# An fp32 encoder trunk: first products without the wait for lambda constants, first weight chunks rounded on ScalarE, and output additions each followed by a square addition and a split

## What is computed

```
h = _rms(x, attn_norm[l])
z = h @ w_in[l]
...
lam = (jnp.exp(jnp.sum(lam_q1[l].astype(jnp.float32) * lam_k1[l].astype(jnp.float32)))
       - jnp.exp(jnp.sum(lam_q2[l].astype(jnp.float32) * lam_k2[l].astype(jnp.float32)))
       + lam_init)
y_diff = _diff_attention(dq, dk, dv, lam, diff_subln[l], lam_init)
...
y_mla = _mla_attention(q_nope, q_pe, k_nope, k_pe, v)

x = x + jnp.concatenate([y_diff, y_mla], axis=-1) @ w_o[l]

h = _rms(x, ffn_norm[l])
x = x + (jax.nn.silu(h @ w_gate[l]) * (h @ w_up[l])) @ w_down[l]
```

## Time and profile before

| | |
|---|---|
| median of 3 runs | 2512.65 us (2512.34 to 2515.03) |
| the profiled execution's own time | 2514.26 us |
| its span in the profile | 2512.5 us |
| mean granted TensorE clock | 0.986 |
| TensorE matmul busy | 2410.7 us, 96% of the span |
| VectorE, ScalarE, GpSimd busy | 1317.1, 564.0, 935.5 us |
| DMA queue q1 | 247.52 MB, 29.1% of 16 engines |

### The profile page before, as it was taken

One profiled execution on the slowest core, in us unless ns is written; L12 is line 12 of the kernel. 1 busy time (PEld: TensorE's weight loads), 2 busy tenths in 40 slices (PEclk: granted clock), 3 DMA queues, 4 the chain that ended last, 5 costly groups with the idle time before them and its releaser, 6 DMA issues.

```text
span 2512.5 us, 31147 instructions
## 1 busy us (share of the span) xinstructions
PE 2410.7 (96%) x11304; PEld 2002.7 (80%) x11304; DVE 1317.1 (52%) x2369; ACT 564.0 (22%) x1089; POOL 935.5 (37%) x798
## 2 busy tenths in 40 slices
PE   5989999989999999999999999999899999999996
PEld 4777788868888888888888888878688888888885
DVE  4898568874333333333359874896533333333335
ACT  2344234520000000000024531453100000000001
POOL 6534300155666666665110010003544343444421
PEclk9999999999999999999999999999899999999998
DMA  7543442232333333332232134223211111111101
GB/s 257 174 145 101 151 151 101 85 118 93 125 126 125 125 125 125 116 114 63 75 112 106 68 126 176 101 84 118 67 42 50 42 50 50 50 50 50 49 18 67
DMA packets 50345, 249.52 MB, mean 99 GB/s; under 512 B 5968, under 2 KB 6096, under 8 KB 32720
## 3 DMA queue, kind: packets, MB, share of 16 engines
q1 hardware_dynamic: 49536, 247.52, 29.1%
q10 hardware_dynamic: 720, 0.86, 0.1%
HBM read 187.54 MB, written 60.82 MB: 99 GB/s over the span
## 4 chain that ended last, share of the span: by engine, by line
PE 87%; DVE 5%; issue 2%; POOL 1%; ACT 0%; DVEq 0%; POOLq 0%; ACTq 0%
PE bank L449 28%; PE bank L451 27%; PE bank L450 27%; PE bank L805 2%; PE bank L668 1%; DVE acc L1150 1%; PE bank L676 1%; DVE aT_lo L1364 1%; DVE qpe L1243 1%; PE bank L456 0%; PE bank L455 0%; DVE y_out L1440 0%; ACT aT_hi L1030 0%; DVE ms L1185 0%; DVE mx L1356 0%
## 5 line engine op out<-in xcount | busy, mean ns | idle before, releaser
L449 PE MATMUL bank<-h_hi,w 128*128 128x512 f32 x1792 | 704.9, 393 | 2.6 <-issue 1.7
L451 PE MATMUL bank<-h_hi,w 128*128 128x512 f32 x1792 | 700.3, 391 | 0.0
L450 PE MATMUL bank<-h_lo,w 128*128 128x512 f32 x1792 | 700.1, 391 | 0.0
L574 POOL TENSOR_TENSOR w<-raw,zero 128x512 fp32r<-128x512 f32 x318 | 335.8, 1077 | 814.6 <-PE bank L451 756.9
L579 POOL TENSOR_TENSOR w<-raw,w 128x512 fp32r<-128x512 f32 x318 | 416.3, 1330 | 12.5
L449 PEld LDWEIGHTS bank<-h_hi,w 128*128 128x128 f32 x1792 | 338.4, 189 | 72.9 <-issue 3.8
L451 PEld LDWEIGHTS bank<-h_hi,w 128*128 128x128 f32 x1792 | 338.0, 189 | 71.3
L450 PEld LDWEIGHTS bank<-h_lo,w 128*128 128x128 f32 x1792 | 338.5, 189 | 69.4
L1408 DVE TENSOR_TENSOR x<-x,bank 128x512 f32<-128x512 f32 x352 | 239.9, 687 | 187.2 <-PE bank L451 184.1
L449 PE MATMUL bank<-u_hi,w 128*128 128x512 f32 x704 | 273.9, 389 | 0.0
L450 PE MATMUL bank<-u_lo,w 128*128 128x512 f32 x704 | 273.9, 389 | 0.0
(11 more groups left out here) (162 smaller groups left out, 3331.6 us busy)
## 6 DMA issues: line engine op xcount, KB each, us to landing
w<-parked SPq DMA_DIRECT2D x81, 1024.0 KB, 4.8
raw<-in_wffn SPq DMA_DIRECT2D x132, 512.0 KB, 3.5
parked<-w SPq DMA_DIRECT2D x27, 1024.0 KB, 6.4
parked<-p SPq DMA_DIRECT2D x27, 1024.0 KB, 4.8
raw<-in_watt SPq DMA_DIRECT2D x27, 512.0 KB, 4.3
praw<-in_watt SPq DMA_DIRECT2D x27, 512.0 KB, 5.7
out_yT<-y_out SPq DMA_DIRECT2D x16, 256.0 KB, 2.3
x<-in_xT SPq DMA_DIRECT2D x4, 512.0 KB, 6.7
```

What stands on the lines that cost most here:

```text
L449: nc.tensor.matmul(out_ap, lhs[0], rhs[0], start=first, stop=False)
L450: nc.tensor.matmul(out_ap, lhs[0], rhs[1], start=False, stop=False)
L451: return nc.tensor.matmul(out_ap, lhs[1], rhs[0], start=False, stop=last)
L574: last = nc.gpsimd.tensor_tensor(w[slot][0][:, cols], src[:, cols], zeros_like(src[:, cols]), ALU.add)
```

## The change

It has three parts.

1. TensorE's wait for s_load and for the set-up is taken from before V of layer 0, input 0, and put behind it, ahead of its first sums; it now asks s_pre for 2 (the ones and the zero) and not for the constants.
2. ScalarE rounds chunks 0, 1 and 2 (`first_hi`), behind x_hi of tiles 1, 3 and 7, and does all 8 squares after that. GpSimd only makes their lo parts. VectorE does all 8 x_lo first, and then the 8 square additions.
3. In input 1 of both layers VectorE does, behind each addition ob(k), k = 1 to 7, `square_add` and `x_lo` of tile k-1. Behind the table only those of tile 7 are left.

```diff
-            for c in (s_hi, s_lo, s_add):
+            for c in (s_lo, s_add):
...
-            def split(j, slot, raw_at, hi_at):
+            def split(j, slot, raw_at, hi_at, rounded=False):
...
-                for n, cols in enumerate(spans(2)):
-                    last = nc.gpsimd.tensor_tensor(w[slot][0][:, cols], src[:, cols], zeros_like(src[:, cols]), ALU.add)
-                last.then_inc(s_hi.sem, 1)
+                if not rounded:
+                    for n, cols in enumerate(spans(2)):
+                        last = nc.gpsimd.tensor_tensor(w[slot][0][:, cols], src[:, cols], zeros_like(src[:, cols]), ALU.add)
+                    last.then_inc(s_hi.sem, 1)
...
-                split(j, j % WS_ATT, s_raw[j % RAW].half_at(0, 0, j // RAW), s_hi.half_at(0, 0, j))
+                split(j, j % WS_ATT, s_raw[j % RAW].half_at(0, 0, j // RAW), s_hi.half_at(0, 0, j), j < 3)
...
-            pe.wait_ge(s_load, 4 * 16)
-            pe.wait_ge(s_pre, PRE_DVE)
...
                             values(l, b)
+                            if l == 0 and b == 0:
+                                pe.wait_ge(s_load, 4 * 16)
+                                pe.wait_ge(s_pre, 2)
...
+            def first_hi(j):
+                act.wait_ge(s_raw[j % RAW].sem, s_raw[j % RAW].half_at(0, 0, j // RAW))
+                for cols in spans(2):
+                    last = nc.scalar.activation(w[j][0][:, cols], raw[:, j % RAW, cols], ACT.Copy)
+                last.then_inc(s_hi.sem, 1)
+
             for k in range(KT):
                 x_hi("first", 0, 0, k)
+                if k in (1, 3):
+                    first_hi(k // 2)
+            first_hi(2)
+            for k in range(KT):
                 norm_square("first", 0, 0, k)
...
             for k in range(KT):
                 x_lo("first", 0, 0, k)
+            for k in range(KT):
                 square_add("first", 0, k)
...
                             add_output(l, b, what)
+                            if b == 1 and what[1] == "b" and what != "ob0":
+                                square_add("last", l, int(what[2]) - 1)
+                                x_lo("last", l, 0, int(what[2]) - 1)
...
-                for k in range(KT):
-                    square_add("last", l, k)
-                    x_lo("last", l, 0, k)
+                square_add("last", l, KT - 1)
+                x_lo("last", l, 0, KT - 1)
```

## The result

| | before | changed |
|---|---|---|
| median | 2512.49 us (2510.4 to 2515.03, 4 runs) | 2490.03 us (2487.16 to 2490.61, 4 runs) |
| ratio to before | | 0.9909, 95% interval 0.9897 to 0.9921 |
| the profiled execution's own time | 2514.26 us | 2487.16 us |
| its span | 2512.5 us | 2485.4 us |
| mean granted TensorE clock | 0.986 | 0.989 |

The kernel is 22.5 us faster. I had forecast about 2475, which is 37.5 less, with a range of 2468 to 2484: the sign is right, the size is not, and the time lies outside the range.

What follows compares the result with a forecast made beforehand. TensorE, busy 2410.7 of 2512.5 us, was taken to bound the kernel, with three stalls totalling 53.3 us. Gains of 18.0 + 9.9 + 9.9 = 37.8 took 2514.3 to 2476.5, the median to about 2475; range 2468 to 2484.

Steps and rivals of the forecast that it cites:

- The start: Kernel start: TensorE begins near 12.4 instead of 30.4 us, and the first sums come at 36.4; gain 18.0 us.
- rival 3: Start: chunks 3 and 4 land late, TensorE stands 2 to 4 us and pays 2.3 of clock; 2480, chance 0.08.
- the sum: Whole kernel: 18.0 us from the start plus 9.9 from each of two hand-overs, 37.8 in all.
- The lag of VectorE: Hand-overs: interleaved work makes the last output addition 2.4 us late, so TensorE stands 3.3 us before the FFN's first product.
- rival 2: Hand-overs: VectorE lags 5.7 us, stall 6.6, gain only 6.6 each, total 31; 2481, chance 0.14.
- The low clock behind them: Hand-overs: after the stall before the FFN's first product the clock falls, costing 2.3 us over the 48 products.
- The step that failed: Hand-overs: sums at once, 0.9, then 24 products, 5.4, to 564.0 instead of 573.83; gain 9.9 us each.
- Rival 1: Hand-overs: the clock doesn't fall at the FFN's start; gain 12.2 each, total 42.4, 2470, chance 0.17.
- Rival 4: Hand-overs: TensorE waits before each ob product at 1.2 GHz, losing 17.4 us per hand-over; slower, 2531, chance 0.02.

Runs made afterwards that it cites:

- e1: The change, with GpSimd held before the FFN's chunk 4 of each layer until the second input's inverse root is made; 2474.93 us, ratio 0.9854.
- e2: The kernel before with parts 1 and 2 of the change alone, hand-overs as before; 2495.82 us, ratio 0.9937.
- e5: e1 with the square additions and splits of tiles 5 to 7 left behind ob7; 2467.72 us, ratio 0.9815.
- e9: e5 with GpSimd also held before chunk 6 of the first input until the first norm's root is made; 2466.91 us, ratio 0.9821.
- e6: e1 with the second input's x loaded with chunk 8 instead of chunk 2; 2475.07 us, ratio 0.9842.
- e4b: The kernel before, with GpSimd's lo part of the FFN's chunk 5 made five times in step 0 of each layer; 2522.16 us against 2514.4.
- e8: e5 and e6 together, with GpSimd held before chunk 6 of the first input until the first norm's root is made; 2464.4 us, ratio 0.9806.

## Why the prediction was wrong

**The start: right, with one term mis-sized.** TensorE began at 12.18 (I had 12.4). ScalarE's two roundings took 1.13 (1.2). The first sums came at 37.93, not 36.4: chunk 3 took 10.2 us to land, not the 7.0 that I borrowed from the load issued at 18.72, and TensorE stood 1.7 before its group (8.7 to 9.7 us, and 0.6 to 0.9, in e1, e2, e5 and e9). The profile puts GpSimd's wait there down to the store of chunk 0; but that store was issued at 12.53 and took 7.9, to 20.4, while the load, 17.14 plus 10.2, ended at 27.3, just when GpSimd began. In e6, with 5.8 for the load, GpSimd began at 22.7, just behind 16.77 plus 5.8. That was rival 3's trigger, at a small price. In all the start brought 16.8 us by e2 against the 18.0 of the sum.

**The lag of VectorE: right.** The addition ob7 started at 524.49, 16.6 earlier than at 541.05, while the step ahead of the lag was 18.8 earlier: 2.2 us late, where I had walked to 2.4 and rival 2 to 5.7. With these 18.8 put back, ob4 to ob7 started at 534.1, 537.0, 539.9 and 543.3; walked were 534.1, 537.0, 540.0 and 543.5. The stalls were 3.1 and 3.3, for a forecast of 3.3. The low clock behind them cost 1.2 us over the 48 products (12.34 from 525.27 to 537.61, against 11.1), and 1.5 in layer 1, where I had 2.3. The Trainium skill's lock ("SBUF — State Buffer", "SBUF: two separate sides") priced this well: the addition with a bank as an operand stayed at 0.67 beside GpSimd.

**The step that failed** is the end of that sum: "sums at once [...], 0.9; 24 products, 5.4, to 564.0", with "rsqrt and the spread keep their places behind the sums". They kept their place in the order and not their price. I moved the sums forward by 7 us and took the root behind them at its old length, at no cost to TensorE, though the same paragraph has that GpSimd's chunks would come "by 564 at worst", that is, through the whole of the root's new place. The same turns that I charged to the square additions met ten of the root's 13 small instructions (rows at 538.86 to 549.18 above), and the one of GpSimd in front lasts 1.0 to 1.3 us. I had not carried the turns on to the root. The trace of before even had it, at the first norm, where GpSimd was splitting:

```profile
55.61 1.02 DVE L1180 TENSOR_SCALAR eps_var<-ms 128x4 f32<-128x4 f32 x1
...
58.05 1.21 DVE L1185 TENSOR_TENSOR ms<-yy 128x4 f32<-128x4 f32 x1
...
56.69 2.56 POOL L579 TENSOR_TENSOR w<-raw,w 128x512 fp32r<-128x512 f32 x2
```

Three instructions at 1.02 to 1.21 among ten at 0.16, with a split of GpSimd's from 54.57 to 59.25 over them. There TensorE had enough products to go on with. At the next norm it had not: the root from 280.45 had five long instructions and took 7.2 us, and TensorE stood 2.45 us for it, in the trace of before and in every other.

```profile
280.64 1.21 DVE L1180 TENSOR_SCALAR eps_var<-ms 128x4 f32<-128x4 f32 x1
...
287.70 1.12 PE L676 MATMUL bank<-ident,rstd 128*128 128x128 f32 x4 [2.45 <-DVE rstd L1187]
```

At the hand-over of layer 0, 13 instructions of 0.88 us on average make a root of 11.5; less the 5.4 of products beside it, that leaves a wait of 6, and the clock falls again. So the two hand-overs brought 2.4 plus 5.8 instead of 19.8. Once the root is kept clear of GpSimd, the sum nearly holds: e1 gains 10.9 and 10.8 where I had 9.9, mostly because the low clock behind the stall cost 1.2 and not 2.3. That e1 comes to 2474.9, the forecast's own number, is in part luck: this surplus offsets a start that is 1.2 short by e2.

**The rivals.** None of the four had this. Rival 1 did not come: the clock fell behind both stalls. Its ground, that a stall of 2.17 us ends at the higher level and one of 3.26 at the lower, was thin, since in the trace of before the granted clock also fell behind the stall of 1.20 us at 261.66. Rival 2 came nearer in gain (31 us) than my sum, by the wrong mechanism, and its 2481 was still 9 off. Rival 4, slower, needed waits before the ob products; there were none over 0.3 us. Its 2531 also starts from the profiled execution and not from the median; by its own terms it is about 2530.

## What to carry to other kernels

When work is pulled forward on one engine, everything behind it moves too, and must be priced against its new neighbours, not its old ones. A chain of many tiny dependent instructions on VectorE is fragile in a stretch where GpSimd works without a pause: here ten of 13 links paid for most of an instruction of the other engine. Look for such a chain elsewhere in the trace beside the same neighbour, and hold the background engine for the length of the chain where it has slack: 6.3 and 6.5 us of waiting on GpSimd saved 15 here.

## What the runs showed of the hardware that I had not expected

- An instruction of VectorE on 128 x 4 elements took 0.16 us alone and 0.85 to 1.22 where it met GpSimd's 128 x 512 splits at the change's hand-overs, five to seven times as much. This held for tensor_tensor and for tensor_scalar with one SBUF tensor, but not for the one that reads a bank (0.16 at 564.26 in e4b, with GpSimd at work from 563.43).
- The clock can fall after TensorE has gone back to work. In layer 1 the stall of 3.28 us was followed by three products at the full clock, and then by some eight at the low one, with a granted clock of 0.50:

```profile
1735.55 0.47 PE L449 MATMUL bank<-h_hi,w 128*128 128x512 f32 x1 [3.28 <-issue]
...
1736.63 0.63 PE L450 MATMUL bank<-h_lo,w 128*128 128x512 f32 x1
...
1736.60:1739.60 3.00, 3.00 (x8) 2.30 (x7) 3.00 (x3) 0.12 (x1) 3.00 (x3) 0.50 0.00 0
```

- Stalls of the same length and at the same place were followed by either level: behind 1.20 us the granted clock was 0.52 in the trace of before and 1.00 in the change's, worth 1.6 us.
- A load of 512 KB issued at 16.6 to 17.1 us took 8.7 to 10.2 us with 2 MB of another tensor issued just ahead of it (the change, e1, e2, e5, e9), and 5.8 and 5.5 without (e6, e8).
